# Raw feed-forward weights split sooner, zeros on TensorE at the start, and part of the causal mask moved to GpSimd

## Chip, cores and metric

The kernel runs on one NeuronCore of a Trainium2 chip. The metric is the device time of one execution in microseconds (us), as the median of several runs.

## What is computed

One layer of a hybrid encoder on 1024 tokens of width 1024, with 16 learned meta tokens in front (1040 rows), all in float32:

```python
hn = rmsnorm(h, mix_norm_g)
q, k, v, ca, cg = split(hn @ w_in)            # 512 columns each
# stick-breaking attention, 8 heads of 64, key s of query t only where s < t:
A[t, s] = sigmoid(z_ts) * prod_{s<j<t} (1 - sigmoid(z_tj))      # z = q.k / 8
conv = silu(layernorm(depthwise_conv31(ca * sigmoid(cg))))
h = h + concat(attn, conv) @ w_out
hn = rmsnorm(h, ffn_norm_g)
h = h + (silu(hn @ w_gate) * (hn @ w_up)) @ w_down              # D_FF = 2816
out = rmsnorm(h, final_norm_g)                # meta tokens dropped
```

## The kernel before

Every matmul of the large products is made of three passes on float32r halves: each operand is split into a high half (ScalarE copies it to the narrower type) and a low half (the rest, a subtraction on VectorE or GpSimd), and high x high, high x low and low x high are added up. The engines run instruction streams written out by hand, which meet at semaphores; the order in each stream is the order of the lists below.

**Start.** GpSimd makes the constants (identity, mask). TensorE spreads the norm's factors g1 over the partitions (L1540), then goes through nine tiles of tokens: VectorE normalises one (L1151), TensorE transposes it (L1550), ScalarE evacuates the high half (L779), VectorE the low one (L1158), and TensorE projects the values of the tile before last (L1570).

**Pairs.** The eight heads are taken as four pairs, p = 0 to 3. In a pair the projections of k and q are finished, then 16 units (head, block of 128 queries) are gone through in the order of the list `UNITS`; unit n has 144 to 1040 keys. `scores(n)` on TensorE multiplies q and k into PSUM (L1660) and, for the block on the diagonal, adds a mask of -1e30 above the diagonal by one more matmul (identity x `mask_bf`, bf16, L1665). ScalarE turns the scores into gates, sigmoid(-z), in one of five buffers `gq` (L917), up to four units ahead. VectorE scans the gates of the unit from the last key to the first as a running product (`tensor_tensor_scan`, L1291); between the scans it makes steps of the depthwise convolution, called taps (L1212, one a unit from n = 9 on in the first three pairs, from n = 7 on in the last). TensorE transposes the scanned rows (L1677), ScalarE copies them (L926), and TensorE multiplies them with differences of the values (L1692). A masked score gives a gate of 1. When the units are done, TensorE goes on with the next pair's projections (L1613). GpSimd's only work in the pairs is the low half of each projection weight (`lo_weight`, L587), which it takes in the order of the list `WEIGHTS`.

**Output projection and feed-forward.** The feed-forward works on 11 chunks of 256 columns; a chunk has a gate block and an up block (b = 0 to 21), each 7 products of a Strassen-like scheme (L1808), numbered 1 to 7 and run in the order `IN_TURN` = 1, 5, 6, 2, 7, 3, 4, and then a down product of 96 matmuls (L1829). The order on TensorE is down(c), up block of chunk c+1, gate block of chunk c+2, down(c+1). A block's weights are loaded into one buffer `raw` as four quarters (SyncE, L514). Products 1, 2 and 4 use a quarter as it stands; 5, 6, 3 and 7 use sums of quarters, which GpSimd makes (L660, L663, L666, L669). ScalarE makes the high halves (`weight_hi`, L1008), GpSimd the low ones (`weight_lo`, L645), in the orders `HI_ORDER` and `LO_ORDER`, which for blocks from 2 on both follow `LATER`. There are six slots for weights, so a product's weights can be written when the product six places before has been made. The next block's load waits until the low half (b, 4) and all four sums of the block have been made:

```python
sp.wait_ge(flo_done, LO_NTH[b - 1, 4] + 1)
sp.wait_ge(s_summed, 4 * b)
```

In a chunk's up block VectorE makes, for the quarters C11, C22, C12 and C21 in turn, the product of gate and up (L1465), and behind the next quarter's product the low half of the one before (`act_low`, L1469). down(c) waits for three of the four low halves, and for the fourth at its eighth tile.

Of the kernel before, what the change touches and what calls it, by code (L numbers as in the profile page):

```python
# [8 lines left out]
BF16 = mybir.dt.bfloat16  # L9
# [8 lines left out]
def hybrid_block(nc, x, meta_tokens, mix_norm_g, w_in, conv_dw_w, conv_dw_b, conv_ln_g, conv_ln_b,  # L18
# [50 lines left out]

    UNITS = [(0, 1), (0, 2), (0, 0), (1, 0), (0, 7), (1, 1), (1, 7), (1, 2),  # L70
# [51 lines left out]
    with ctx:  # L122
# [64 lines left out]
        mask_bf = keep("mask_bf", [P, P], BF16)  # L187
        par = keep("par", [P, 4, NP], F32)
# [47 lines left out]
        consts, par_t, par_ready = sem("consts"), sem("par_t"), sem("par_ready")  # L236
# [13 lines left out]
        z_ready, z_free, scanned = sem("z_ready"), sem("z_free"), sem("scanned")  # L250
# [81 lines left out]


# [4 lines left out]
        PRODUCTS, HI_ORDER, LO_ORDER = FIRST_P + LATER, FIRST_HI + LATER, FIRST_LO + LATER  # L338
# [216 lines left out]
        def _(pool):  # L555
# [70 lines left out]
            for kind, p in WEIGHTS[4:]:  # L626
                lo_weight(kind, p)
# [78 lines left out]
            def block_weights(b):  # L706
                weight_lo(b, 1)
                weight_sum(b, 5)
                weight_sum(b, 6)
                weight_lo(b, 5)  # L710
                weight_sum(b, 3)
                weight_lo(b, 6)
                weight_lo(b, 2)
                weight_sum(b, 7)
                weight_lo(b, 7)
                weight_lo(b, 3)
                weight_lo(b, 4)
# [419 lines left out]
        def _(dve):  # L1137
            dve.sem_inc(conv_step, 1)
# [127 lines left out]
            def pair(p, more):  # L1266
# [19 lines left out]
                for n, (h, i) in enumerate(UNITS):  # L1286
                    w = width(i)

                    dve.wait_ge(z_free, past(NZ * p + CZ[n + 1]))
                    gates = gq[:, n % BUFS, 0:w][:, ::-1]  # L1290
                    dve.tensor_tensor_scan(out=gates, data0=gates, data1=ones_row(w),  # L1291
                                           initial=1.0, op0=ALU.mult, op1=ALU.mult).then_inc(scanned, 1)
                    if n == HELD_BACK - 1:
                        if not more:
                            step_values(p)
                        split_lo("q", 1, p)
                    if more and (n == 0 or n > 8):
                        some_taps(p + 1, ahead, 1)
                    elif not more and n > 6:
                        some_taps(p, now, 1)  # L1300
                    if not more and NU - 5 <= n < NU - 1:
                        w_out_lo(n - NU + 5)
                    if n == NU - 2 and not more:
                        spread(p, 0)
# [179 lines left out]
            def up_block(c):  # L1484

                b = 2 * c + 1
                if c:
                    addition(b, "U4")
                    addition(b, "C11")
                product(c, "C11")  # L1490
                if c == 0:
                    addition(0, "C22")
                    addition(0, "C12")
                    addition(1, "U4")
                behind = "C11"
                for q in IN_ORDER[1:]:
                    if q != "C21":
                        addition(b, q)
                    product(c, q)
                    act_low(c, behind)  # L1500
                    behind = q
                act_low(c, behind)
# [31 lines left out]
        def _(pe):  # L1534
            for s in (z_ready, t_ready, pv_used):
                pe.sem_inc(s, 1)
            pe.wait_ge(consts, 10)
            pe.wait_ge(g1_loaded, 16)
            for b in range(2):
                pe.matmul(ps[:, PJ + b, :], ones_1[:, :], g1row[:, b * BANK:(b + 1) * BANK],  # L1540
                          start=True, stop=True).then_inc(g1_spread, 1)

# [92 lines left out]
            def pair(p, behind):  # L1635
# [7 lines left out]
                def scores(n):  # L1643
# [9 lines left out]
                    for c, (c0, cols, used) in enumerate(z_chunks(i)):  # L1653
# [5 lines left out]
                        for part in range(2):  # L1659
                            last = pe.matmul(ps[:, Z_BANKS[m], 0:cols], qst[:, h, i * P:(i + 1) * P],  # L1660
                                             kd[:, h, part, c0:c0 + cols], start=(part == 0),
                                             stop=(part == 1 and c0 + used <= d0))
                        lo, hi = max(d0, c0), c0 + used
                        if hi > lo:
# [238 lines left out]
```

## Time and profile before

| | us |
|---|---|
| median of 3 runs (lowest, highest) | 1189.51 (1189.15, 1190.39) |
| the profiled execution | 1190.92 |
| its span, first to last instruction | 1189.2 |
| TensorE busy | 1159.6 (98%) |
| TensorE weight loads busy | 987.0 (83%) |
| VectorE busy | 689.3 (58%) |
| GpSimd busy | 483.9 (41%) |
| ScalarE busy | 431.2 (36%) |

The span is the time that the profile covers; the execution adds what lies around it. A matmul's end is modelled from the pipeline, so TensorE that is busy by this table can still have short gaps between the starts of its matmuls. In the profile PE is TensorE, PEld its weight loads, DVE VectorE, ACT ScalarE, POOL GpSimd, SP SyncE; L and a number is the line of the kernel. The shares are averages over stages with different limits.

### The profile page before, as it was taken

The page shows a single profiled execution, that of the slowest core. Times are in us where ns is not written, and L with a number is a line of the kernel's source. Part 1 is how long each engine was busy: PE and PEld are TensorE (multiplying, and loading weights), DVE is VectorE, ACT ScalarE, POOL GpSimd, SP SyncE. Part 2 cuts the span into 40 slices and gives each one's busy share as a digit, 9 for nine tenths or more (in the row PEclk, how much of TensorE's full clock was granted, in tenths as well). Part 3 has the DMA queues.
Part 4 walks back from the last instruction along what each step waited for, and adds up shares of the span by engine and source line. Part 5 has one row for each costly group of instructions (what it writes and reads, how often), then busy time and mean ns, then how long its engine had stood idle before and what let it go on. Part 6 is the DMA issues. An engine that isn't in the chain of part 4 may idle for free.

```text
span 1189.2 us, 15351 instructions
## 1 busy us (share of the span) xinstructions
PE 1159.6 (98%) x5944; PEld 987.0 (83%) x5944; DVE 689.3 (58%) x744; ACT 431.2 (36%) x875; POOL 483.9 (41%) x370
## 2 busy tenths in 40 slices
PE   8999999999999999989999999999999999999997
PEld 6899899899898888768878787878787888888786
DVE  5339998998998656684343443434434343433347
ACT  6321553533737644453231313132222222221323
POOL 4116112202200023377364655556564647373822
PEclk9999999999999999999999999999999999999999
DMA  7203312203026011122111112121212121212114
GB/s 261 80 10 96 74 47 71 73 16 81 13 59 217 19 50 39 36 71 71 36 41 52 50 36 71 36 71 37 71 37 71 36 71 36 71 36 71 36 36 159
DMA packets 70911, 75.69 MB, mean 64 GB/s; under 512 B 11513, under 2 KB 60149, under 8 KB 70840
## 3 DMA queue, kind: packets, MB, share of 16 engines
q1 hardware_dynamic: 69656, 72.60, 19.7%
q10 hardware_dynamic: 1184, 2.13, 0.5%
q8 instruction: 47, 0.77, 0.3%
q14 instruction: 24, 0.20, 0.1%
HBM read 64.13 MB, written 6.32 MB: 59 GB/s over the span
## 4 chain that ended last, share of the span: by engine, by line
PE 69%; POOL 12%; DVE 10%; issue 8%; ACT 1%; DMA 0%; POOLq 0%; DVEq 0%; SPq 0%; ACTq 0%
PE ps L1829 20%; PE ps L1808 17%; PE ps L1613 15%; PE ps L1759 7%; DVE gq L1291 6%; PE ps L1570 4%; POOL wa_lo L645 4%; POOL wb_lo L645 2%; DVE acc L1212 2%; POOL wa_f L666 1%; POOL wa_f L660 1%; POOL wa_f L663 1%; PE ps L1692 1%; PE ps L1550 1%; PE ps L1660 1%
## 5 line engine op out<-in xcount | busy, mean ns | idle before, releaser
L1480 DVE TENSOR_TENSOR mix<-ps,mix 128x512 f32<-128x512 f32 x176 | 121.7, 691 | 138.5 <-PE ps L1829 138.5
L1212 DVE SCALAR_TENSOR_TENSOR acc<-u_pad,par,acc 128x1024 f32<-128x1024 f32 x116 | 152.8, 1360 | 1.5 <-ACT acc L836 1.4
L1829 PE MATMUL ps<-wd_hi,act_hi 128*128 128x512 f32 x352 | 137.0, 389 | 1.5 <-DVE act_lo L1469 1.5
L1829 PE MATMUL ps<-wd_hi,act_lo 128*128 128x512 f32 x352 | 136.9, 389 | 0.0
L1829 PE MATMUL ps<-wd_lo,act_hi 128*128 128x512 f32 x352 | 136.9, 389 | 0.0
L645 POOL TENSOR_TENSOR wa_lo<-wa_f,wa_hi 128x512 fp32r<-128x512 f32 x58 | 79.3, 1370 | 133.0 <-ACT wa_hi L1008 129.2
L587 POOL TENSOR_TENSOR wp_lo<-raw,wp_hi 128x1024 fp32r<-128x1024 f32 x16 | 48.9, 3057 | 194.3 <-ACT wp_hi L753 194.3
L1613 PE MATMUL ps<-hn_hi,wp_hi 128*128 128x348 f32 (+2 forms) x352 | 118.7, 337 | 0.0
L1613 PE MATMUL ps<-hn_lo,wp_hi 128*128 128x348 f32 (+2 forms) x352 | 117.7, 334 | 0.0
L1613 PE MATMUL ps<-hn_hi,wp_lo 128*128 128x348 f32 (+2 forms) x352 | 117.5, 334 | 0.0
L1291 DVE TENSOR_TENSOR_SCAN gq<-gq,ones 128x1040 f32<-128x1040 f32 (+4 forms) x64 | 98.1, 1562 | 4.5 <-ACT gq L917 4.4
L1808 PE MATMUL ps<-t_hi,wa_hi 128*128 128x512 f32 x232 | 91.9, 396 | 6.5 <-POOL wa_lo L645 6.4
L1808 PE MATMUL ps<-t_lo,wa_hi 128*128 128x512 f32 x232 | 90.4, 390 | 0.0
L1808 PE MATMUL ps<-t_hi,wa_lo 128*128 128x512 f32 x232 | 90.3, 389 | 0.0
L1057 ACT ACTIVATE act_f<-ps 128x512 f32<-128x512 f32 x22 | 13.1, 598 | 210.7 <-PE ps L1808 210.7
L645 POOL TENSOR_TENSOR wa_lo<-raw,wa_hi 128x512 fp32r<-128x512 f32 x44 | 58.8, 1337 | 59.0 <-ACT wa_hi L1008 59.0
L1829 PEld LDWEIGHTS ps<-wd_hi,act_hi 128*128 128x128 f32 x352 | 66.1, 188 | 15.6 <-DVE act_lo L1469 1.9
L1829 PEld LDWEIGHTS ps<-wd_lo,act_hi 128*128 128x128 f32 x352 | 66.1, 188 | 13.7
L1829 PEld LDWEIGHTS ps<-wd_hi,act_lo 128*128 128x128 f32 x352 | 66.1, 188 | 13.7
L1692 PE MATMUL ps<-w_t,vs_of 128*128 128x128 f32 x576 | 75.0, 275 | 0.0
L1808 PE MATMUL ps<-b_hi,wa_hi 128*128 128x512 f32 x180 | 70.9, 394 | 2.6 <-DVE b_lo L1360 1.8
L1808 PE MATMUL ps<-b_hi,wa_lo 128*128 128x512 f32 x180 | 70.7, 393 | 0.0
(187 smaller groups left out, 2627.1 us busy)
## 6 DMA issues: line engine op xcount, KB each, us to landing
raw<-in_w_gate SPq DMA_DIRECT2D x11, 1024.0 KB, 5.3
raw<-in_w_up SPq DMA_DIRECT2D x11, 1024.0 KB, 5.3
wd_f<-in_w_down SPq DMA_DIRECT2D x11, 1024.0 KB, 4.9
raw<-in_w_in SPq DMA_DIRECT2D x16, 512.0 KB, 3.9
xin<-in_x SPq DMA_DIRECT2D x8, 512.0 KB, 10.0
wo_raw<-in_w_out SPq DMA_DIRECT2D x4, 1024.0 KB, 8.4
mix<-in_x SPq DMA_DIRECT2D x8, 512.0 KB, 3.7
out<-ost SPq DMA_DIRECT2D x7, 512.0 KB, 2.6
```

What stands on the lines that cost most here:

```text
L587: pool.tensor_tensor(dst, raw[:, slot, :], hi.bitcast(F32), ALU.subtract).then_inc(wlo_done, 1)
L645: pool.tensor_tensor(w_lo_of(n), src, w_hi_of(n).bitcast(F32), ALU.subtract).then_inc(flo_done, 1)
L1057: act.activation(cell(act_f if b % 2 else sil, q), ps[:, x_ if k == 1 else y_, :], ACT.Copy).then_inc(c_copied, 1)
L1212: dve.scalar_tensor_tensor(out=acc[:, j % 2, :], in0=u_pad[:, p % 2, j:j + L], scalar=par[:, p, j:j + 1], in1=acc[:, j % 2, :], op0=ALU.mu ...
L1291: dve.tensor_tensor_scan(out=gates, data0=gates, data1=ones_row(w), initial=1.0, op0=ALU.mult, op1=ALU.mult).then_inc(scanned, 1)
L1480: dve.tensor_tensor(hrow, ps[:, TB + n % 4, :], hrow, ALU.add).then_inc(d_added, 1)
L1570: last = pe.matmul(ps[:, PV + b % 2, :], hn[s][:, k, c0:c0 + P], wv[m][:, k, :], start=(n == 0), stop=(n == 3 * KD - 1))
L1613: last = pe.matmul(ps[:, bank, 0:n], w_[s][:, slot, k, :], hn[m][:, k, c0:c0 + n], start=(k == 0 and s == m == 0), stop=(k == KD - 1 and s ...
L1692: last = pe.matmul(ps[:, PV + i // 4, (i % 4) * P:(i % 4 + 1) * P], vs_of[:, kb, h, :], w_t[:, m % 4, j, :], start=(kb == 0 and n == first ...
L1759: last = pe.matmul(ps[:, (PJ, PV)[i % 2] + dh, :], ms[s][:, k, :], wo[m][:, 4 * part + k, dh * BANK:(dh + 1) * BANK], start=(part == 0 and ...
L1808: last = pe.matmul(ps[:, bank, :], w[s][:, j, :], tokens[k][m][:, j, :], start=(k not in (6, 7, 4) and j == 0 and s == m == 0), stop=(j == ...
L1829: last = pe.matmul(ps[:, TB + n % 4, :], a[s][:, t, i * P:(i + 1) * P], w_[m][:, t, dh * BANK:(dh + 1) * BANK], start=(t == 0 and s == m = ...
```

## The change

1. `LATER_W` is a new order for the high and low halves of blocks 2 to 21: 1, 5, 6, 2, 4, 7, 3. The order of the products, and with it the slots, stays. GpSimd's (b, 4) low half stands ahead of those of (b, 7) and (b, 3).
2. In the last chunk VectorE makes the low half of C12 before the product of C21.
3. VectorE clears a tile `idle` (128 x 512, bf16) first of all, and TensorE multiplies it with itself three times before the constants are awaited, and seven times behind the two g1 products. The results go to a bank that is overwritten later.
4. For the units n = 5 to 15 of each pair the mask matmul is left out; GpSimd sets the masked gates of the diagonal block to 1 in the buffer with an `affine_select`, and VectorE's scan waits for it. GpSimd's weight low halves are ordered around the masks: three of a pair's before mask 5, one behind mask 6.

```diff
+    BY_SELECT = 5
+        idle = keep("idle", [P, BANK], BF16)
...
+        LATER_W = [(b, k) for b in range(2, BLOCKS) for k in (1, 5, 6, 2, 4, 7, 3)]
...
-        PRODUCTS, HI_ORDER, LO_ORDER = FIRST_P + LATER, FIRST_HI + LATER, FIRST_LO + LATER
+        PRODUCTS, HI_ORDER, LO_ORDER = FIRST_P + LATER, FIRST_HI + LATER_W, FIRST_LO + LATER_W
...
-            for kind, p in WEIGHTS[4:]:
-                lo_weight(kind, p)
+            def mask(p, n):
+
+                d0 = META + UNITS[n][1] * P
+                pool.wait_ge(z_free, past(NZ * p + CZ[n + 1]))
+                pool.affine_select(out=gq[:, n % BUFS, d0:d0 + P], in_=gq[:, n % BUFS, d0:d0 + P], compare_op=ALU.is_ge,
+                                   fill=1.0, base=-1, pattern=[[-1, P]], channel_multiplier=1).then_inc(z_masked, 1)
+
+            for p in range(PAIRS):
+                for kind, q in WEIGHTS[4 + 4 * p:7 + 4 * p]:
+                    lo_weight(kind, q)
+                for n in range(BY_SELECT, NU):
+                    mask(p, n)
+                    if n == BY_SELECT + 1:
+                        for kind, q in WEIGHTS[7 + 4 * p:8 + 4 * p]:
+                            lo_weight(kind, q)
...
                 weight_sum(b, 7)
+                weight_lo(b, 4)
                 weight_lo(b, 7)
                 weight_lo(b, 3)
-                weight_lo(b, 4)
...
         def _(dve):
+            dve.memset(idle[:, :], 0.0).then_inc(idle_ready, 1)
...
                     dve.wait_ge(z_free, past(NZ * p + CZ[n + 1]))
+                    if n >= BY_SELECT:
+                        dve.wait_ge(z_masked, (NU - BY_SELECT) * p + n - BY_SELECT + 1)
...
-                    product(c, q)
-                    act_low(c, behind)
+                    if q == "C21" and c + 1 == CHUNKS:
+                        act_low(c, behind)
+                        product(c, q)
+                    else:
+                        product(c, q)
+                        act_low(c, behind)
...
+            def keep_busy(n):
+
+                for _ in range(n):
+                    pe.matmul(ps[:, PV, :], idle[:, 0:P], idle[:, :], start=True, stop=True)
+
+            pe.wait_ge(idle_ready, 1)
+            keep_busy(3)
             pe.wait_ge(consts, 10)
...
+            keep_busy(7)
...
-                                             stop=(part == 1 and c0 + used <= d0))
+                                             stop=(part == 1 and (n >= BY_SELECT or c0 + used <= d0)))
                         lo, hi = max(d0, c0), c0 + used
-                        if hi > lo:
+                        if hi > lo and n < BY_SELECT:
```

## Rows read from the trace of the kernel before

**Rows 1.** The page, shares of the chain that ended last, by engine.
```profile
PE 69%; POOL 12%; DVE 10%; issue 8%; ACT 1%; DMA 0%; POOLq 0%; DVEq 0%; SPq 0%; ACTq 0%
```

**Rows 2.** Busy time by window; the columns end with clock, DMA share and GB/s.
```profile
core 0: us, PE busy (x) PEld busy (x) DVE busy (x) ACT busy (x) POOL busy (x), PEclk, DMA share, GB/s
144.60:172.40 27.80, 27.63 (x232) 25.84 (x231) 27.80 (x19) 19.05 (x55) 4.44 (x1) 1.00 0.21 56
```

**Rows 3.** The chain, end of the first pair's units: start, duration, what.
```profile
170.88 1.45 DVE gq L1291
...
172.37 0.77 PE ps L1677 x5
```

**Rows 4.** Who TensorE waited for from 553 us on: total, times, longest.
```profile
PE ps L1808 <- POOL wa_lo L645: 5.0, 9, 1.3
PE ps L1808 <- POOL wb_lo L645: 2.6, 4, 1.4
```

**Rows 5.** Timeline of TensorE around one such wait: start, duration, [idle before].
```profile
859.01 0.39 PE L1808 MATMUL ps<-t_hi,wa_lo 128*128 128x512 f32 x1
859.77 0.50 PE L1808 MATMUL ps<-t_hi,wa_hi 128*128 128x512 f32 x1 [0.38 <-POOL wa_lo L645]
860.11 0.40 PE L1808 MATMUL ps<-t_lo,wa_hi 128*128 128x512 f32 x1
```

**Rows 6.** Busy time by window, one period of the feed-forward.
```profile
798.80:859.70 60.90, 60.42 (x264) 49.39 (x264) 24.47 (x32) 16.25 (x28) 34.36 (x26) 1.00 0.16 52
```

**Rows 7.** The chain at the start.
```profile
8.77 1.98 PE ps L1550 x8
```

**Rows 8.** Timeline of the first 30 us, TensorE and VectorE.
```profile
20.10 1.22 DVE L1158 TENSOR_TENSOR hn_lo<-ps,hn_hi 128x1024 fp32r<-128x1024 f32 x1
...
22.31 0.48 PE L1570 MATMUL ps<-wv_hi,hn_hi 128*128 128x512 f32 x1
...
27.96 1.03 PE L1550 MATMUL ps<-ident,xnorm 128*128 128x128 f32 x8
```

**Rows 9.** Timeline of GpSimd and of SyncE's queue, an up block's end.
```profile
838.46 1.28 POOL L645 TENSOR_TENSOR wb_lo<-wb_f,wb_hi 128x512 fp32r<-128x512 f32 x1 [16.01 <-ACT wb_hi L1008]
...
849.90 1.30 POOL L645 TENSOR_TENSOR wb_lo<-raw,wb_hi 128x512 fp32r<-128x512 f32 x1 [6.19 <-ACT wb_hi L1008]
...
843.74 0.37 SPq L514 DMA_DIRECT2D raw<-in_w_gate  x1
```

**Rows 10.** Timeline of VectorE and TensorE ahead of the last down.
```profile
1159.12 0.69 DVE L1465 TENSOR_TENSOR act_f<-sil,ps 128x512 f32<-128x512 f32 x1 [0.66 <-PE ps L1808]
...
1160.47 0.50 PE L1829 MATMUL ps<-wd_hi,act_hi 128*128 128x512 f32 x1 [1.45 <-DVE act_lo L1469]
```

**Rows 11.** The mask's line, 144 to 172 us: ns min/median/max, first and last start.
```profile
L1665 PE MATMUL ps<-mask_bf,ident_bf x11: 229/229/230, 143.8 to 164.7; 128*128 128x128 bf16 x11
```

**Rows 12.** Timeline of GpSimd, the two other selects of this shape.
```profile
100.44 10.70 POOL L616 TENSOR_SCALAR_AFFINE_SELECT own<-own 128x128 f32<-128x128 f32 x1
111.20 0.34 POOL L620 TENSOR_SCALAR_AFFINE_SELECT own<-own 128x128 f32<-128x128 f32 x1
```

**Rows 13.** Timeline of VectorE in that time.
```profile
95.30 15.62 DVE L1212 SCALAR_TENSOR_TENSOR acc<-u_pad,par,acc 128x1024 f32<-128x1024 f32 x13
110.85 0.51 DVE L1187 TENSOR_TENSOR u_pad<-ps,u_pad 128x348 f32<-128x348 f32 x1
```

**Rows 14.** Timeline of GpSimd and VectorE: a weight split among the scans.
```profile
147.47 4.44 POOL L587 TENSOR_TENSOR wp_lo<-raw,wp_hi 128x1024 fp32r<-128x1024 f32 x1 [8.58 <-ACT wp_hi L753]
...
149.66 3.09 DVE L1291 TENSOR_TENSOR_SCAN gq<-gq,ones 128x400 f32<-128x400 f32 x1
...
140.57 0.98 DVE L1291 TENSOR_TENSOR_SCAN gq<-gq,ones 128x400 f32<-128x400 f32 x1
```

**Rows 15.** Timeline, a hand-over from GpSimd to VectorE.
```profile
399.35 0.56 POOL L633 TENSOR_TENSOR ln_rstd<-ln_var,half 128x1 f32<-128x1 f32 x1
...
399.94 0.81 DVE L1334 TENSOR_SCALAR mix<-ps,bn,ln_rstd 128x512 f32<-128x512 f32 x1 [0.95 <-POOL ln_rstd L633]
```

**Rows 16.** Timeline of ScalarE, the gates of unit 12.
```profile
157.36 0.89 ACT L917 ACTIVATE gq<-ps 128x392 f32<-128x392 f32 x2 [1.55 <-PE ps L1660]
```

More of the change, by code:

```diff
@@ L235, in hybrid_block @@
         wv_loaded, wvhi_done, wvlo_done = [sem(f"wv_loaded{j}") for j in range(4)], sem("wvhi_done"), sem("wvlo_done")
-        consts, par_t, par_ready = sem("consts"), sem("par_t"), sem("par_ready")
+        consts, idle_ready, par_t, par_ready = sem("consts"), sem("idle_ready"), sem("par_t"), sem("par_ready")
         x_sumsq, x_var, x_rstd, xn_ready = sem("x_sumsq"), sem("x_var"), sem("x_rstd"), sem("xn_ready")
@@ L249, in hybrid_block @@
         u_zeroed, conv_first, conv_step = sem("u_zeroed"), sem("conv_first"), sem("conv_step")
-        z_ready, z_free, scanned = sem("z_ready"), sem("z_free"), sem("scanned")
+        z_ready, z_free, z_masked, scanned = sem("z_ready"), sem("z_free"), sem("z_masked"), sem("scanned")
         t_ready, t_copied, pv_used, pv_evac = sem("t_ready"), sem("t_copied"), sem("pv_used"), sem("pv_evac")
```

## The prediction

> **What bounds the kernel now.** I read the page, then the chain and the busy windows of each stage, then the waits and the timelines. The page's chain of work that ended last says: TensorE holds 69% of it, GpSimd 12%, VectorE 10% [rows 1]. So saved work on another engine pays only where that engine's link in the chain is, and I looked at each place that the diff touches for the link there.
>
> Attention. In the first pair's stretch from 144.6 to 172.4 us VectorE is busy 27.80 of 27.80 us [rows 2]; the chain runs scan, tap, scan, and its last scan (170.88 + 1.45 = 172.33) hands over to the transposes at 172.37 [rows 3]. TensorE runs without much of a gap too, but it is the one that waits at the end. Every microsecond that VectorE loses here comes out at the end of the pair, four times.
>
> Feed-forward. TensorE is the chain, but 13 times it waits for a low half from GpSimd, 7.6 us as printed [rows 4]. The printed idle is too small, since a matmul's end is modelled: at 859.77 the view prints 0.38, but the start before is 859.01, and starts in a stream are 0.23 apart, so 0.53 is lost, and 0.11 more because the next start comes 0.34 later [rows 5]. So add 0.26 a time: 7.6 + 13 x 0.26 = 11.0 us. That's the prize. One period of two blocks and a down takes 60.90 us there, another the same [rows 6].
>
> Start. Eight transposes take 1.98 us at 8.77 and 1.03 us at 27.96 [rows 7, 8]: TensorE begins at half speed (1.2 of 2.4 GHz by the durations; the clock column prints 1.00 there, so it is the durations that I go by).
>
> **1. Raw quarters split sooner (blocks 2 to 21).** The same instructions in another order. In a block the (b, 4) low half is the last reader of raw; behind it SyncE issues the next load at 843.74, and GpSimd works on it from 849.90 [rows 9]. Its high half needs the slot that product (b, 1) frees, and that is what ScalarE waits for anyway just before the piece that GpSimd now splits at 838.46. So (b, 4) takes that place, raw is free at 838.46 + 1.28 = 839.74, and the load starts 4.0 us earlier. The waits that hang on it are 7.6 us printed over 9 periods with 13 waits, 1.2 us a period with the 0.26 added, and the longest is 1.4 [rows 4]: two in a row still fit within 4.0. What is late next: (b, 7) and (b, 3) each move back one place. The clock for that: a product is 12 x 0.227 = 2.72 us; product (b+1, 6) starts at 859.77 with two waits of together 0.9 ahead of it, so would start at 858.9, and nine products before, at 834.4, is (b, 1). (b, 7) now waits for one product more: 838.46 + 2.72 + 1.28 = 842.5, and its product starts at 834.4 + 4 x 2.72 = 845.3: covered. The sum that makes (b+1, 3) needs the slot of (b, 4), free at 834.4 + 7 x 2.72 = 853.4, so GpSimd is stopped there, and (b+1, 6), with 1.8 for the sum and 1.6 for itself, is ready at 856.8: covered by 2 us. SyncE's order of loads doesn't change, and the down weights are requested after the raw ones as before. Value: -11.0. Bounds: -3 (only the second waits go, as if the load were late for another reason) and -12.
>
> **2. Last chunk: low half before the last product.** Down starts at 1160.47 and waits for the third low half; ahead of that half VectorE does the C21 product, which waits 0.66 for TensorE's last product and takes 0.69 [rows 10]. In the new order both come behind the low half, which then waits only 0.1 for its high half: 0.66 + 0.69 - 0.1, about 1.2 sooner. Value: -1.2; the C21 quarter is needed only after eight tiles, 11 us later. Bounds: 0 and -1.6.
>
> **3. Zeros on TensorE.** One memset on VectorE, before it has any other work, three matmuls while GpSimd makes the constants, seven in the gap up to 8.77. Should those still be running at half speed at 8.77, they push the first transposes by a few tenths. If the clock is up by then, the first transposes take 1.03 in place of 1.98, and VectorE's chain behind them comes 0.95 earlier. The next full projection needs VectorE's low half at 20.10 + 1.22 = 21.32 and the TensorE work before it, and starts at 22.31 [rows 8]. With TensorE at full level its own queue is done by 20.4, and the low half too (21.32 - 0.95), so it starts 1.9 earlier. From there TensorE is the bound and carries that on. Value: -1.9. Bounds: +0.3 (nothing lifts the clock) and -2.8. The Trainium skill (TensorE: Matmul & The Clock Gate, Part 1) says that the engine starts throttled and activity releases it; whether multiplying zeros counts as such no run here shows.
>
> **4. The mask on the gates.** Removed: 11 matmuls a pair, 0.23 us each as printed, some 0.06 in the stream, a quarter of 512 columns' 0.23 [rows 5, 11], so 44 x 0.06 = 2.6 us of TensorE, none of it on the path, since TensorE waits at the end. Added: 11 affine_selects a pair on GpSimd, in place, 128 x 128, and VectorE's scan waits for each. Queued behind a waiting scan are taps, further scans and then TensorE's transposes. Alone such a select takes 0.34 us; but the one issued at 100.44 took 10.70 [rows 12]. In that time VectorE ran taps end to end, and the select ended only after VectorE's instruction at 110.85, the first that takes one input from PSUM, had begun [rows 13]. So I read it as shut out by back-to-back VectorE instructions with two SBUF inputs, past eight gaps between them. Scans have two SBUF inputs too, and they collide: the scan of 400 columns takes 3.09 where GpSimd's subtraction (issued 147.47) got in, and 0.98 otherwise [rows 14].
>
> If masks are shut out, one goes through only when VectorE stands still at a scan's wait. Price of a stop: the select ends 0.21 after the last tap (111.14 against 110.92), the hand-over takes 0.03 or more (399.91 to 399.94) [rows 15], and the usual overlap of 0.07 is lost: about 0.36. The next unit's gates are ready well before (unit 12's at 157.36 + 0.89 = 158.25, while its scan starts four VectorE instructions later than the one then running) [rows 16], so GpSimd goes straight into the next mask before the scan begins, holding it up some 0.15, half a select. So units 5/6, 7/8, 9/10, 11/12, 13/14 cost 0.5 a couple and unit 15 0.36: 2.9 us a pair, 11.4 in all. Bounds: 11 single stops of 0.45, 20 us; and 0.1 for each mask, 4.4 us. Below nothing is excluded, because VectorE, full in that stretch, only gets waits. The last pair has no weight split there but the same 11 masks.
>
> What speaks against this change most is a rule of the Trainium skill (SBUF — State Buffer, Who interferes with whom): a VectorE instruction with two SBUF inputs and a GpSimd one that reads SBUF exclude each other for a whole instruction, whichever is issued first. The collision in rows 14 agrees; the 10.70 us doesn't, for there a later instruction went first eight times. By the Trainium skill's rule the term would be 7 us in place of 11.4 (the first rival), and the sum -7.1.
>
> **Sum.** -11.0 - 1.2 - 1.9 + 11.4 = -2.7. The profiled execution took 1190.92 us, of which the span is 1189.2; that gives 1188.2, and since it lies 1.4 above the median of the runs, 1186.8 for the median, say 1187.
>
> **Rivals.**
> - *Masks slip in between.* GpSimd wins the gap after each instruction, as its subtraction did at 149.66, so only the masks up to unit 9, which have no tap between scans, cost a stop. 5 x 0.3 + 6 x 0.05 = 1.8 a pair, 7 in all: 1182.5. For: rows 14; against: rows 12. The Trainium skill's rule named above, which lets a waiting select in at the first gap, makes it this case.
> - *Every mask a stop of its own (slower).* The scan takes the lock before the second mask does, so 11 stops a pair of 0.4: 17.6 us, and the time is 1193. It decides from nine lone stops a pair on (9 x 4 x 0.4 = 14.4 eats the gains of 14.1). For: a select lost eight gaps in a row; against: GpSimd starts the next select 0.07 behind the first, about when the scan starts.
> - *Zeros lift nothing.* The start gains nothing or loses 0.3: 1189.
> - *The sooner split doesn't act.* The load starts sooner but lands no sooner, or the stopped sum holds GpSimd up: part 1 gives 3 in place of 11, and the time is 1195. Against: TensorE, SyncE and GpSimd all stand in one line of waits there.
>
> **How the numbers follow.** Forecast 0.42 (1187, own range 1184 to 1190), slip in between 0.20, lone stops 0.20, zeros lift nothing 0.10, split doesn't act 0.08. The bound for a difference is 0.2%, 2.4 us, about what a measurement of this kernel can tell from no change. Faster (under 1187.1): 0.26 of the forecast's, 0.20, and 0.04 of the zeros case: 0.50. Slower (over 1191.9): 0.20, 0.08 and 0.01: 0.29. Same: 0.21. The range runs from the slip-in case to the lone stops, 1182 to 1194; beyond lie the split that doesn't act and masks at their dearest.
>
> **What would show it.** Feed-forward: no waits for low halves, and a period of 60.0 in place of 60.9 us; each raw load 4 us sooner after the block's first product. End: a gap below 0.6 ahead of the last down. Start: first transposes in 1.0, the second full projection at about 20.4. Attention: VectorE waits for masks printed at its scans, about six a pair, and a stretch of about 30.7 us in place of 27.8. Selects of 1 to 3 us mean that they were shut out; 0.3 to 0.5 means that they slipped in. I am wrong if the stretch grows by less than 1.5 or more than 4, or if a feed-forward wait stays.

## The result and the profile after

| | before | after |
|---|---|---|
| median (lowest to highest), us | 1189.88 (1189.15 to 1190.39), 4 runs | 1180.76 (1179.95 to 1181.45), 4 runs |
| profiled execution, span | 1190.92, 1189.2 | 1180.64, 1178.9 |

The ratio is 0.9924, with a 95% interval of 0.9906 to 0.9941: 9.1 us faster. The forecast was 1187, with a range of 1182 to 1194, so the time is below the range. The traces are read in the prediction's order of parts. Chain of the page of after, shares by engine (answers to [rows 1]):

```profile
PE 63%; issue 4%; POOL 4%; DVE 3%; ACT 0%; POOLq 0%; DVEq 0%; ACTq 0%
```

These shares add up to 74% only: the chain followed back from the end breaks off at 313.77 us, so nothing of the start and of the first two pairs is in it, and VectorE's 3% can't be set beside the 10% of before. The same line of the first experiment below (all masks back on TensorE) is whole:

```profile
PE 83%; DVE 10%; POOL 3%; issue 2%; ACT 1%; POOLq 0%; DVEq 0%; ACTq 0%
```

There VectorE has its 10% as before, and GpSimd has fallen from 12% to 3%; the 4% above agrees with that, since the feed-forward lies in the part that is followed. Then the waits of TensorE from 553 us on (total, times, longest), which answer to [rows 4]:

```profile
PE ps L1841 <- POOL wa_lo L663: 0.4, 1, 0.4
PE ps L1862 <- DVE act_lo L1490: 0.3, 1, 0.3
```

Of the 13 waits for low halves one is left. An up block and what follows it show why (L1841 are the products, L1862 the down). The fences answer to [rows 6, 9]. TensorE's timeline, the block's first product:

```profile
830.67 0.39 PE L1841 MATMUL ps<-b_hi,wa_hi 128*128 128x512 f32 x1
```

The block's first product in the trace of before:

```profile
834.35 0.39 PE L1808 MATMUL ps<-b_hi,wa_hi 128*128 128x512 f32 x1
```

SyncE's queue, the next load:

```profile
836.09 0.37 SPq L519 DMA_DIRECT2D raw<-in_w_gate  x1
```

GpSimd's timeline, the low halves (b, 4) and (b, 7) and then the sum at which it is stopped:

```profile
834.78 1.28 POOL L663 TENSOR_TENSOR wa_lo<-raw,wa_hi 128x512 fp32r<-128x512 f32 x1 [19.64 <-ACT wa_hi L1026]
837.50 1.29 POOL L663 TENSOR_TENSOR wb_lo<-wb_f,wb_hi 128x512 fp32r<-128x512 f32 x1 [1.44 <-ACT wb_hi L1026]
...
849.95 1.37 POOL L684 TENSOR_TENSOR wa_f<-raw,wa_f 128x512 f32<-128x512 f32 x1 [1.73 <-PE ps L1841]
```

Busy time by window, one period from first product to first product:

```profile
830.67:890.80 60.13, 60.10 (x265) 49.47 (x264) 27.20 (x32) 16.72 (x28) 34.65 (x24) 1.00 0.16 53
```

The load of the next raw block is issued 836.09 - 830.67 = 5.42 us after the block's first product. Before it was issued at 843.74 [rows 9], 9.39 after the first product at 834.35. So it comes 3.97 us sooner. The period is 60.13 us in place of 60.92, and TensorE is busy for 60.10 of it. Measured from down to down, six of the nine full periods of after take 59.84 us and three 60.07 to 60.13. Before, six took 60.67 to 60.92 and three 62.01 to 62.24. From the first down to the last one the trace of before has 1160.47 - 566.82 = 593.65 us, and that of after 1150.17 - 569.55 = 580.62: 13.03 less.

Attention, first pair. The next fences answer to [rows 2, 14]. Busy time from the first scan of 1040 columns to the end of the last scan:

```profile
143.60:172.30 28.70, 27.12 (x220) 25.96 (x219) 28.32 (x19) 18.91 (x55) 16.08 (x12) 1.00 0.21 54
```

VectorE's waits in it (total, times, longest):

```profile
DVE gq L1312 <- POOL gq L635: 0.4, 2, 0.2
```

VectorE's scans in it, by shape (count, then busy us and mean ns):

```profile
L1312 DVE TENSOR_TENSOR_SCAN gq<-gq,ones 128x1040 f32<-128x1040 f32 x2 | 6.7, 3372 | 0.8 <-ACT gq L935 0.8
L1312 DVE TENSOR_TENSOR_SCAN gq<-gq,ones 128x912 f32<-128x912 f32 x2 | 4.1, 2060 | 0.0
L1312 DVE TENSOR_TENSOR_SCAN gq<-gq,ones 128x784 f32<-128x784 f32 x2 | 3.6, 1823 | 0.0
L1312 DVE TENSOR_TENSOR_SCAN gq<-gq,ones 128x656 f32<-128x656 f32 x2 | 3.1, 1558 | 0.0
L1312 DVE TENSOR_TENSOR_SCAN gq<-gq,ones 128x528 f32<-128x528 f32 x2 | 2.6, 1306 | 0.0
L1312 DVE TENSOR_TENSOR_SCAN gq<-gq,ones 128x400 f32<-128x400 f32 x1 | 1.0, 991 | 0.2 <-POOL gq L635 0.2
```

VectorE waits for a mask twice in that stretch, not six times. The stretch takes 28.70 us; before it took 172.32 - 144.59 = 27.73. From the first scan of all to the last scan's end the trace of before has 257.15 us, and that of after 260.86: 3.71 more. GpSimd's timeline in the stretch:

```profile
143.99 2.26 POOL L635 TENSOR_SCALAR_AFFINE_SELECT gq<-gq 128x128 f32<-128x128 f32 x2 [6.11 <-ACT gq L935]
146.33 2.66 POOL L592 TENSOR_TENSOR wp_lo<-raw,wp_hi 128x1024 fp32r<-128x1024 f32 x1
148.94 6.69 POOL L635 TENSOR_SCALAR_AFFINE_SELECT gq<-gq 128x128 f32<-128x128 f32 x5
```

And VectorE's:

```profile
143.59 2.33 DVE L1312 TENSOR_TENSOR_SCAN gq<-gq,ones 128x1040 f32<-128x1040 f32 x1 [0.77 <-ACT gq L935]
146.10 5.07 DVE L1312 TENSOR_TENSOR_SCAN gq<-gq,ones 128x272 f32<-128x272 f32 x2 [0.19 <-POOL gq L635]
151.36 4.18 DVE L1312 TENSOR_TENSOR_SCAN gq<-gq,ones 128x400 f32<-128x400 f32 x3 [0.19 <-POOL gq L635]
```

The scan that starts at 143.59 ends at 145.92, and the first select at 146.00: it waited 1.9 us for that end. The second goes through right behind it in 0.29, while VectorE, stopped by the first, starts up again. The next five take 6.69 us, in which VectorE has four ends: again one select waits for each end, and one uses the stop at 151.2. Over all four pairs VectorE stops for a mask seven times, twice in each of the first three and once in the last. No select is passed over for long: of the 44, 41 have at most one end of a VectorE instruction between their own start and end, and the other three started 0.03 us ahead of an end and took the next one.

Start: TensorE's timeline, which answers to [rows 7, 8]:

```profile
6.35 3.17 PE L1565 MATMUL ps<-idle 128*128 128x512 bf16 x7
9.31 1.92 PE L1583 MATMUL ps<-ident,xnorm 128*128 128x128 f32 x16
...
14.41 1.09 PE L1583 MATMUL ps<-ident,xnorm 128*128 128x128 f32 x8
...
20.14 1.09 PE L1583 MATMUL ps<-ident,xnorm 128*128 128x128 f32 x8 [0.47 <-DVE xnorm L1170]
21.28 0.50 PE L1603 MATMUL ps<-wv_hi,hn_hi 128*128 128x512 f32 x1
```

The first tile is normalised by 7.25 + 1.29 = 8.54 us, but its transposes start only at 9.31, behind the zeros. Both first tiles (the second has only 16 rows) then take 1.92 us, where they took 3.01 before, 1.98 of it the first [rows 7]. The second full projection starts at 21.28, not 22.31 [rows 8].

The last down answers to [rows 10]. TensorE's last product before the change:

```profile
1158.63 0.39 PE L1808 MATMUL ps<-t_hi,wb_lo 128*128 128x512 f32 x1
```

And after it, with the first matmul of the down:

```profile
1149.50 0.39 PE L1841 MATMUL ps<-t_hi,wb_lo 128*128 128x512 f32 x1
1150.17 0.50 PE L1862 MATMUL ps<-wd_hi,act_hi 128*128 128x512 f32 x1 [0.28 <-DVE act_lo L1490]
```

The starts of the last product and of the down are 0.67 us apart, 0.23 of it the matmul itself, so 0.44 is lost. Before it was 1160.47 - 1158.63 = 1.84, so 1.61.

**The difference by stage, from the two traces.** First scan of all 136.86 to 135.85: -1.01. From it to the end of the last scan +3.71. From the last scan to the first down 172.81 to 172.84: 0. Between first and last down -13.03, of which the last chunk is 0.44 - 1.61 = -1.17 and the rest -11.86. Sum -10.3, and the spans say 1178.9 - 1189.2 = -10.3.

### The profile page after: what moved, and what is told of

Its sections match the earlier page's. It is cut to its first block, busy times and chain, and to the rows that moved or that the text cites. A ratio compares the mean times of both kernels' runs of the same rounds, so it can differ in the third digit from the quotient of the medians.

```text
span 1178.9 us, 15416 instructions
## 1 busy us (share of the span) xinstructions
PE 1154.8 (98%) x5910; PEld 987.5 (84%) x5910; DVE 706.8 (60%) x745; ACT 436.4 (37%) x875; POOL 533.4 (45%) x414
## 4 chain that ended last, share of the span: by engine, by line
PE 63%; issue 4%; POOL 4%; DVE 3%; ACT 0%; POOLq 0%; DVEq 0%; ACTq 0%
PE ps L1841 31%; PE ps L1862 20%; PE ps L1792 7%; PE ps L1646 2%; DVE gq L1312 1%; POOL wa_lo L663 1%; POOL wb_lo L663 1%; DVE acc L1231 1%; PE ps L1725 0%; DVE wo_lo L1254 0%; PE ps L1805 0%; POOL gq L635 0%; PE ps L1775 0%; PE ps L1768 0%; POOL wa_f L687 0%
## 5 line engine op out<-in xcount | busy, mean ns | idle before, releaser
L1862 PE MATMUL ps<-wd_hi,act_hi 128*128 128x512 f32 x352 | 137.1, 389 | 0.3 <-DVE act_lo L1490 0.3
L1862 PE MATMUL ps<-wd_hi,act_lo 128*128 128x512 f32 x352 | 136.9, 389 | 0.0
L1862 PE MATMUL ps<-wd_lo,act_hi 128*128 128x512 f32 x352 | 136.9, 389 | 0.0
L663 POOL TENSOR_TENSOR wa_lo<-raw,wa_hi 128x512 fp32r<-128x512 f32 x44 | 61.5, 1398 | 142.3 <-ACT wa_hi L1026 142.3
L592 POOL TENSOR_TENSOR wp_lo<-raw,wp_hi 128x1024 fp32r<-128x1024 f32 x16 | 43.6, 2724 | 142.4 <-ACT wp_hi L771 142.2
L1841 PE MATMUL ps<-t_hi,wa_hi 128*128 128x512 f32 x232 | 90.6, 391 | 1.7 <-POOL wa_lo L663 1.7
L1841 PE MATMUL ps<-t_hi,wa_lo 128*128 128x512 f32 x232 | 90.3, 389 | 0.0
L1841 PE MATMUL ps<-t_lo,wa_hi 128*128 128x512 f32 x232 | 90.3, 389 | 0.0
L635 POOL TENSOR_SCALAR_AFFINE_SELECT gq<-gq 128x128 f32<-128x128 f32 x44 | 51.8, 1189 | 82.2 <-ACT gq L935 82.0
L1862 PEld LDWEIGHTS ps<-wd_hi,act_hi 128*128 128x128 f32 x352 | 66.1, 188 | 14.5 <-DVE act_lo L1490 0.7
L1862 PEld LDWEIGHTS ps<-wd_hi,act_lo 128*128 128x128 f32 x352 | 66.1, 188 | 13.7
L1862 PEld LDWEIGHTS ps<-wd_lo,act_hi 128*128 128x128 f32 x352 | 66.1, 188 | 13.7
L1841 PE MATMUL ps<-b_hi,wa_hi 128*128 128x512 f32 x180 | 71.1, 395 | 2.7 <-DVE b_lo L1381 1.8
```

Of the source, the lines that this page charges most:

```text
L592: pool.tensor_tensor(dst, raw[:, slot, :], hi.bitcast(F32), ALU.subtract).then_inc(wlo_done, 1)
L635: pool.affine_select(out=gq[:, n % BUFS, d0:d0 + P], in_=gq[:, n % BUFS, d0:d0 + P], compare_op=ALU.is_ge, fill=1.0, base=-1, pattern=[[-1 ...
L663: pool.tensor_tensor(w_lo_of(n), src, w_hi_of(n).bitcast(F32), ALU.subtract).then_inc(flo_done, 1)
L1841: last = pe.matmul(ps[:, bank, :], w[s][:, j, :], tokens[k][m][:, j, :], start=(k not in (6, 7, 4) and j == 0 and s == m == 0), stop=(j == ...
L1862: last = pe.matmul(ps[:, TB + n % 4, :], a[s][:, t, i * P:(i + 1) * P], w_[m][:, t, dh * BANK:(dh + 1) * BANK], start=(t == 0 and s == m = ...
```

## The experiments

The kernel before was measured again beside them, with medians of 1189.84 to 1189.97 us (one run of 1189.11 beside the two last). Ratios are to the kernel before.

**All masks on TensorE.** The changed kernel without part 4.

```diff
-    BY_SELECT = 5
+    BY_SELECT = 16
...
-                for kind, q in WEIGHTS[4 + 4 * p:7 + 4 * p]:
+                for kind, q in WEIGHTS[4 + 4 * p:8 + 4 * p]:
...
-                    if n == BY_SELECT + 1:
-                        for kind, q in WEIGHTS[7 + 4 * p:8 + 4 * p]:
-                            lo_weight(kind, q)
```

> The changed kernel with all masks back on TensorE. Theory (a mask on GpSimd costs VectorE's full stretch, but little: it slips in at instruction ends, about 0.93 us a pair by the two traces): each pair's stretch of scans falls from 28.7 to 27.7 us, the time by 3.7 us to about 1177. Rival (the mask matmuls taken off TensorE pay for themselves somewhere else in the pair): the time stays within 1 us of 1180.8 or rises. Second rival (masks cost 2.9 us a pair as I had forecast, and something else gave back 8 us): about 1169.

Measured: 1177.18 us (1176.59 to 1177.32), ratio 0.9890 [0.9876, 0.9903]. So the theory holds, and part 4 costs 3.6 us. Busy time in the first pair's stretch:

```profile
144.17:171.90 27.73, 27.59 (x231) 25.80 (x229) 27.73 (x19) 19.08 (x55) 4.45 (x1) 1.00 0.21 56
```

Its scans by shape:

```profile
L1309 DVE TENSOR_TENSOR_SCAN gq<-gq,ones 128x1040 f32<-128x1040 f32 x2 | 4.6, 2312 | 0.8 <-ACT gq L932 0.8
L1309 DVE TENSOR_TENSOR_SCAN gq<-gq,ones 128x912 f32<-128x912 f32 x2 | 4.1, 2037 | 0.0
L1309 DVE TENSOR_TENSOR_SCAN gq<-gq,ones 128x784 f32<-128x784 f32 x2 | 3.6, 1780 | 0.0
L1309 DVE TENSOR_TENSOR_SCAN gq<-gq,ones 128x400 f32<-128x400 f32 x1 | 3.1, 3093 | 0.0
L1309 DVE TENSOR_TENSOR_SCAN gq<-gq,ones 128x656 f32<-128x656 f32 x2 | 3.0, 1514 | 0.0
L1309 DVE TENSOR_TENSOR_SCAN gq<-gq,ones 128x528 f32<-128x528 f32 x2 | 2.5, 1236 | 0.0
```

The stretch is 27.73 us again, and this fence beside that of after, shape by shape, gives the price. The scans of 912, 784, 656 and 528 columns are 23, 43, 44 and 70 ns longer with the selects, two of each: 0.36 us. The weight split's collision only moves from the scan of 400 to one of 1040 (together 3093 + 2 x 2312 = 7717 ns, after 991 + 2 x 3372 = 7735). The two stops are 0.19 printed and the lost overlap of about 0.08 each: 0.54. Together 0.9 of the 0.97 us by which the stretch grew. The means hide a pattern that shows when the two traces are laid side by side, instruction by instruction, over all four pairs. Where a select has ended just after VectorE's next instruction began, that instruction takes 0.04 to 0.05 us longer if it is a scan behind another scan (1.27 in place of 1.23 at 154.27), 0.09 if it is a scan behind a tap (1.34 in place of 1.25 at 159.79), and nothing if it is a tap (1.25 at 155.47, with and without).

**The mask alone.** The kernel before with part 4, nothing else; the tile `idle` has its place in memory and isn't used. Against the changed kernel:

```diff
-        LATER_W = [(b, k) for b in range(2, BLOCKS) for k in (1, 5, 6, 2, 4, 7, 3)]
+        LATER_W = [(b, k) for b in range(2, BLOCKS) for k in IN_TURN]
...
-                weight_lo(b, 4)
                 weight_lo(b, 7)
                 weight_lo(b, 3)
+                weight_lo(b, 4)
...
-            dve.memset(idle[:, :], 0.0).then_inc(idle_ready, 1)
...
-                    if q == "C21" and c + 1 == CHUNKS:
+                    if False:
...
-            pe.wait_ge(idle_ready, 1)
-            keep_busy(3)
...
-            keep_busy(7)
```

> The kernel before with the mask part alone. Theory (0.93 us a pair, independent of the rest): 3.7 us slower than before, about 1193.6. Rival (the forecast's price of 2.9 us a pair, hidden in the full change by the earlier start or another phase of the engines): about 1201. Second rival (the mask part pays by itself): not slower than before.

Measured: 1192.80 us (1191.8 to 1193.96), ratio 1.0024 [1.0015, 1.0033], 2.9 us slower, where 3.7 was expected. From the first scan to the end of the last it takes 261.10 us, 3.95 more than before. So part 4 costs about the same without the other parts, far from the 11 us of the rival, and what it takes from TensorE pays nowhere.

**The masks of units 9 to 15 on GpSimd, those of 5 to 8 back on TensorE.**

```diff
-    BY_SELECT = 5
+    BY_SELECT = 9
```

> The changed kernel with the masks of units 9 to 15 alone on GpSimd; those of units 5 to 8 are back on TensorE. Theory (the two stops of 0.3 us at units 5 and 7 are gone, and a mask that slips in costs VectorE 0.05 to 0.1): 0.3 to 0.5 us a pair are left over the kernel with no mask on GpSimd, so 1178.4 to 1179.2. Rival (the price is per mask and the same for all): 7/11 of 3.7, about 1179.6. Second rival (with a tap between the scans masks cost nothing): 1177.2.

Measured: 1178.42 us (1176.88 to 1179.05), ratio 0.9901 [0.9885, 0.9918]. Busy time in the stretch:

```profile
144.17:172.07 27.90, 27.24 (x224) 25.93 (x223) 27.90 (x19) 18.89 (x55) 10.85 (x8) 1.00 0.21 57
```

Seven masks cost this pair 27.90 - 27.73 = 0.17 us, and VectorE is busy for the whole stretch: no stops. All four pairs together lose 0.9 us, and the medians say 1.2. The masks of units 5 to 8, whose scans follow each other without a tap, cost the other 0.8 of a pair, so the price is not the same for every mask.

**The old order of the low and high halves.**

```diff
-        LATER_W = [(b, k) for b in range(2, BLOCKS) for k in (1, 5, 6, 2, 4, 7, 3)]
+        LATER_W = [(b, k) for b in range(2, BLOCKS) for k in IN_TURN]
...
-                weight_lo(b, 4)
                 weight_lo(b, 7)
                 weight_lo(b, 3)
+                weight_lo(b, 4)
```

> The changed kernel with the old order 1, 5, 6, 2, 7, 3, 4 of high and low halves. Theory (all of the feed-forward gain outside the last chunk is the sooner load of raw): the 13 waits for low halves come back and the time rises by 11.9 us to about 1192.6. Rival (part of the shorter feed-forward comes from another part of the change or from the clock): a rise of clearly less, 3 to 9 us.

Measured: 1191.35 us (1189.88 to 1192.09), ratio 1.0008 [0.9999, 1.0017]. So part 1 is worth 10.6 us, where 11.9 was expected from the two traces. TensorE's waits between the first and the last down:

```profile
PE ps L1841 <- POOL wb_lo L663: 2.5, 4, 1.4
PE ps L1841 <- POOL wa_lo L663: 2.5, 7, 0.4
PE ps L1841 <- ACT wa_hi L1026: 0.6, 2, 0.3
...
PE ps L1841 <- ACT wb_hi L1026: 0.2, 1, 0.2
```

The waits are back, 14 of them, though some now end on ScalarE's high half, which stands in the same line. The load is issued at 846.36, 9.41 us after the block's first product at 836.95. Here one of the nine periods takes over 62 us (62.23), where the trace of before has three, and each is some 1.3 us longer than the rest. So the 11.9 of the traces holds two long periods more than this experiment, and their number differs from trace to trace (two in that of the mask alone).

**The last chunk undone.**

```diff
-                    if q == "C21" and c + 1 == CHUNKS:
+                    if False:
```

> The changed kernel with part 2 alone undone: in the last chunk the product of C21 stands ahead of the low half of C12 again, as before the change. The trace of the changed kernel shows a gap of 0.44 us ahead of the last down where the kernel before had 1.61. Theory A (the prediction's step 2): the low half waits again for TensorE's last product and for VectorE's product, 0.66 + 0.69 less 0.1, so the gap ahead of the last down is about 1.6 again and the time is 1.2 us longer than the changed kernel's, 1181.9. Theory B: another wait, for the act_hi half or the down weights, ends at nearly the same time, so that less than 0.5 us comes back.

Measured: 1181.92 us (1181.7 to 1182.74), ratio 0.9933 [0.992, 0.9947], 1.2 over the changed kernel, as theory A had it. The wait ahead of the last down is the one of [rows 10] again:

```profile
1152.27 0.50 PE L1862 MATMUL ps<-wd_hi,act_hi 128*128 128x512 f32 x1 [1.45 <-DVE act_lo L1490]
```

**No zeros, and five in place of the seven.** Without zeros:

```diff
-            dve.memset(idle[:, :], 0.0).then_inc(idle_ready, 1)
...
-            pe.wait_ge(idle_ready, 1)
-            keep_busy(3)
...
-            keep_busy(7)
```

With five:

```diff
-            keep_busy(7)
+            keep_busy(5)
```

> The changed kernel without the ten zero matmuls and their memset. Theory (they lift the clock at 9.9 in place of 18.1 us, but the last of them overrun the arrival of the first normalised tile by 0.75 us, so only 1.0 is left): 1.0 us slower, about 1181.8, the second full projection at 22.3. Rival (the start is set by the loads, and the zeros did nothing): no difference.

> The changed kernel with five zero matmuls in place of seven behind the g1 products. Theory (seven overrun the first normalised tile by 0.75 us because they run at the lower clock, five end ahead of it, and the clock still rises near 9.9 us): first transposes at about 8.6 in place of 9.3, the second full projection 0.5 to 0.7 earlier, the time about 1180.2. Rival (TensorE must be kept busy right up to the transposes for the clock to rise): the clock rises at 13 us or later, and the time is 1181 to 1182.

Measured: 1181.54 us (1180.28 to 1182.42) without zeros, 1180.36 (1179.84 to 1180.76) with five, 1180.76 with seven; the ranges overlap. TensorE's timeline without zeros:

```profile
15.95 1.85 PE L1579 MATMUL ps<-ident,xnorm 128*128 128x128 f32 x8
```

And with five:

```profile
8.89 2.65 PE L1583 MATMUL ps<-ident,xnorm 128*128 128x128 f32 x16 [0.22 <-DVE xnorm L1170]
...
14.93 1.91 PE L1583 MATMUL ps<-ident,xnorm 128*128 128x128 f32 x8
```

Eight transposes of a whole tile take 1.85 to 1.91 us at half speed (1.2 GHz) and 1.03 to 1.09 at full (2.4). The column of the granted clock prints 1.00 for both, so it is again the durations that tell. Seven zeros do raise the clock earlier. With five it was back at half speed at 14.93, and the second full projection started at 21.55, not sooner than the 21.28 of the changed kernel. The worth in time is small: the first scan of all starts at 136.86, 136.70 and 136.21 us in the three traces without zeros, and at 135.85 to 136.44 (mean 136.2) in the eleven with seven, five or four. That is about 0.4 sooner in the mean, with a scatter of 0.6 within each group, so the worth of the zeros is at the edge of what these runs can tell.

**All masks on TensorE, with five zeros and with four.** The edit of the first experiment, with `keep_busy(5)` and `keep_busy(4)`.

> All masks on TensorE and five zeros: the better version of both, if five zeros pay. Theory: 1177.2 less 0.6, about 1176.6. Rival as for five zeros: 1177.5 to 1178.

> The changed kernel with all masks on TensorE (as in the first experiment) and three plus four zero matmuls in place of three plus seven. With seven the first transposes started at 9.31 us, 0.5 late; with five at 8.76 to 8.89, but the clock fell back to half at 14.1 us in one of two traces. Theory A (the start is bound by VectorE's chain of norms, tile after tile, and the zeros only decide how long the first transposes take): the time is that of the kernels with seven and with five, 1177.1 within 0.5 us. Theory B (the number of zeros matters through the clock): with four the clock rises after the first transposes or not before 15 us, the second full projection starts at 22 us or later, and the time is 1177.6 or more.

Measured: 1176.96 us (1176.01 to 1177.93), ratio 0.9891 [0.9876, 0.9905], and 1176.77 (1176.04 to 1177.75), ratio 0.9890 [0.9877, 0.9904]. With seven it was 1177.18. The three can't be told apart. The clock can: TensorE's timeline with five, in this second trace of that number:

```profile
8.76 3.01 PE L1580 MATMUL ps<-ident,xnorm 128*128 128x128 f32 x16
...
15.59 1.04 PE L1580 MATMUL ps<-ident,xnorm 128*128 128x128 f32 x8
```

The first sixteen transposes take 3.01 us, as without zeros, so here five had not raised the clock by then, and with four it is the same (3.01 at 9.18). For four zeros the second theory was right about the clock and the first about the time: the number matters for the clock and not, within the noise, for the time. These are the fastest versions, 13 us under the kernel before.

**Another GpSimd instruction among the taps.** One instruction on a tile of its own, `trial`, is put ahead of GpSimd's memset of `own`, where VectorE makes taps end to end. First it is a select like that of the masks:

```diff
+        trial = keep("trial", [P, P], F32)
...
+            pool.memset(trial[:, :], 1.0).then_inc(tried, 1)
+            pool.wait_ge(tried, 1)
+            pool.affine_select(out=trial[:, 0:P], in_=trial[:, 0:P], compare_op=ALU.is_ge,
+                               fill=1.0, base=-1, pattern=[[-1, P]], channel_multiplier=1).then_inc(tried, 1)
+            pool.wait_ge(tried, 2)
```

> The changed kernel with one more select on GpSimd, of the masks' very form (128 x 128, one step per column) on a tile of its own, issued among the back-to-back taps ahead of the select that takes 11.8 us. Theory A (a stream of taps shuts a select out, of whatever pattern; between scans and taps it is let in): the new select ends only behind the first VectorE instruction with a PSUM input, near 110, some 11 us long, and the next one is then short. Theory B (the long select is a matter of its own pattern or of its first use): the new one ends behind one tap, in 1.3 us or less, and the old one keeps its 10 us.

Then an add of two inputs, `pool.tensor_tensor(trial, trial, trial, ALU.add)`, and a scaling of one, `pool.tensor_scalar(trial, trial, 2.0, None, ALU.mult)`:

> The changed kernel with one more GpSimd instruction on a tile of its own, a tensor_tensor add of 128 x 128, at the place where the extra select of the experiment before took 11.66 us beside a stream of back-to-back taps. Theory A (it is the stream of taps that shuts GpSimd's reads out, whatever the instruction): the add too ends only after VectorE's instruction with a PSUM input at about 109.4 us has begun, so it takes 10 us or more. Theory B (it is the select that loses, while a tensor_tensor gets in at the first end of a VectorE instruction, as the weight's subtraction did among the scans): it takes 0.3 to 1.5 us.

> As the experiment before, with a tensor_scalar of 128 x 128, which like the select has one input. Theory A (the stream of taps): 10 us or more, until the instruction with a PSUM input at about 109.4 us. Theory B (the select alone loses): 0.3 to 1.5 us. If the add gets in and this one doesn't, it is the single input.

Measured, one run each: 1180.78 us with the select, 1180.51 with the add and 1180.90 with the scaling, no different from the changed kernel's 1180.76. GpSimd's timeline with the select:

```profile
97.67 0.20 POOL L620 MEMSET trial<- 128x128 f32 x1
98.02 11.66 POOL L622 TENSOR_SCALAR_AFFINE_SELECT trial<-trial 128x128 f32<-128x128 f32 x1
...
110.01 1.34 POOL L627 TENSOR_SCALAR_AFFINE_SELECT own<-own 128x128 f32<-128x128 f32 x1
```

With the add:

```profile
98.04 11.83 POOL L622 TENSOR_TENSOR trial<-trial 128x128 f32<-128x128 f32 x1
```

VectorE's timeline beside the add:

```profile
92.78 16.83 DVE L1236 SCALAR_TENSOR_TENSOR acc<-u_pad,par,acc 128x1024 f32<-128x1024 f32 x14
109.53 0.51 DVE L1211 TENSOR_TENSOR u_pad<-ps,u_pad 128x348 f32<-128x348 f32 x1
109.96 2.52 DVE L1236 SCALAR_TENSOR_TENSOR acc<-u_pad,par,acc 128x1024 f32<-128x1024 f32 x2
```

With the scaling:

```profile
98.29 11.96 POOL L622 TENSOR_SCALAR trial<-trial 128x128 f32<-128x128 f32 x1
```

All three end 0.2 to 0.5 us after VectorE's instruction with a PSUM input has begun (add: 109.87 against 109.53). The memset, which only writes, takes 0.20 among the same taps. So it is the long stream of taps that shuts GpSimd's reads out, not the select: theory A, three times. Still, this isn't the whole rule: the select at 110.01 ended at 111.35, behind one tap, with another tap following, and the traces of the add and of the scaling have the same. How many taps stand ahead of the PSUM instruction wasn't varied either. In the fourteen traces a waiting instruction was passed over eight times (three traces) or nine times (eleven), and always ended 0.2 to 0.5 us after the PSUM instruction had begun. That ties the end to that instruction, but it doesn't rule out that some limit near eight or nine has a part in it.

## Why the prediction missed

**1. Raw quarters split sooner: right.** The sum said -11.0; the traces say -11.86 and the experiment that undoes it 10.6. The difference between the two is that of the long periods, told with that experiment. The steps hold too, counted from the block's first product. The load is 3.97 us sooner (4.0 said). (b, 7) is done at 838.79, 8.1 us after that product (842.5 - 834.4 = 8.1 said). GpSimd is stopped at the sum that makes (b+1, 3) until 849.95, 19.3 us after it (19.0 said), and no product waits for what comes behind it. The period of 60.0 was 59.84 to 60.13. Only the period of before was read too narrowly: [rows 6] stands for six of nine, and the other three were 1.3 longer. The statement that no wait for a low half would stay is wrong by one wait of 0.4 us.

**2. Last chunk: right.** -1.2 said, -1.17 in the trace, 1.2 by the experiment.

**3. Zeros: right that they raise the clock, too dear in the sum.** The sum said -1.9. The three traces without zeros and the eleven with them differ by 0.4 in the mean, the medians by 0.8, and neither is clear of the scatter. The step that failed is "VectorE's chain behind them comes 0.95 earlier", and "by 20.4" with it: VectorE's normalising instructions and the low half at 20.00 to 21.22 are 0.1 earlier (20.10 before, [rows 8]), and TensorE, though quicker, still waits 0.47 for a normalised tile at 20.14. The 0.95 that the transposes gain was partly spent on the zeros themselves: they hold up the first transposes by 0.8 us, more than the "few tenths" said.

**4. The mask: the step that failed.** It is the sentence "So I read it as shut out by back-to-back VectorE instructions with two SBUF inputs, past eight gaps between them", and the step from there to the scans. The first half was right for a stream of taps alone, as the added select, add and scaling show. The second half carried it to the units, where a scan follows each tap or another scan, and there a waiting select got in at the next end of an instruction. The subtraction in [rows 14] had already shown it, and the prediction left that row to the rival. A select that slipped in costs the next VectorE instruction nothing if it is a tap, and 0.04 to 0.09 us if it is a scan. It costs a stop of 0.27 where its scan is the very next instruction: seven stops in all, where the prediction had about six a pair. (The prediction's stop of 0.36 was also a little dear for its own terms: 0.21 + 0.03 + 0.07 is 0.31.) So 2.9 us a pair was 0.97, and 11.4 in all was 3.7 in the traces, 3.6 by the experiment. That is below the lower bound of 4.4, which stood at 0.1 for each mask.

The rival *masks slip in between* has the right mechanism, with too many stops: five a pair, where two came and one in the last, since GpSimd gets ahead of VectorE as soon as a select or two are through. The Trainium skill (SBUF — State Buffer, Who interferes with whom) states a rule that fits it: whichever of the two engines issues first has the shared pair of ports for one whole instruction, and the other is blocked meanwhile. The units agree: a select that waits goes at the next end. The 11.66 to 11.96 us among the taps don't: there, later taps went first some nine times.

**The sum with what was measured.** -11.86 - 1.17 - 1.01 + 3.71 = -10.3 in the spans. That is 7.6 us more gain than the -2.7 of the forecast: 7.7 from the mask, 0.9 from the raw quarters and -0.9 from the zeros. That the last two cancel is luck, and what is left of the miss is the mask's price. (In the medians the gain is 9.1 us and not 10.3, because the profiled execution of before lay above its median.)

The other rivals fell: the lone stops (at most two a pair came, not nine or more), the sooner split that doesn't act, and in part the zeros that lift nothing, whose effect on the whole is at the edge of what the traces can tell.

## What to carry to other kernels

A duration taken from one place holds only for the pattern of instructions beside it: before you carry a 10 us collision to another stage, look for an instruction of the same engine that has already been through that stage, and believe that one. Work taken off an engine that waits at the end of a stretch (here TensorE's mask matmuls) pays nothing, and giving it to an engine whose instructions can hold up the one that bounds the stretch costs (here GpSimd and VectorE, 3.6 us), so undo such a part by itself and measure it. A weight buffer's last reader is worth moving forward past pieces that need nothing from the buffer: four microseconds of lead took away waits worth 10.6 us.

## What the runs showed of the hardware

- A stream of scalar_tensor_tensor instructions with two SBUF inputs kept a waiting GpSimd instruction that reads SBUF (select, add or scaling of 128 x 128) out for 10.53 to 11.96 us, past eight or nine ends, until VectorE took an instruction with a PSUM input. A memset of the same size took 0.20 us beside it. Among scans, or scans and taps in turn, a select of the same size waited for one end at most in 41 cases of 44, and for a second in the other three. Why a select could pass between two taps at 111.35 stays open; the order in which the engines ask was not varied.
- Slipping in costs VectorE less than the 0.29 us of the select alone: 0.04 to 0.05 us for a scan behind a scan, 0.09 for a scan behind a tap, nothing for a tap.
- Multiplying zeros in bf16 raised TensorE from its lower to its higher clock before the first real product, by the durations of transposes (the first sixteen 1.92 in place of 3.01, eight later ones 1.09 at 14.41 in place of 1.85 at 15.95). So it was in all eight traces with seven zeros. With five of them it had risen and fallen back by 14.93 in one trace, and in the other, as with four, it had not risen by the end of the first transposes.
